# A fused two-block transformer kernel: x is loaded and normalised ahead of the memory, whose transposes move between the first four token groups

## What is computed

```python
# first block (mixer 0), L = 256 tokens, D = 2048
sh1, sc1, g1, sh2, sc2, g2 = split(silu(c) @ w_mod + b_mod, 6)        # w_mod: 2048 x 12288
h = rms_norm(x, norm_g[0]) * (1 + sc1) + sh1
y = real(fftn(h.reshape(L, 8, 256), axes=(0, 2))) @ fnet_w_out        # Fourier mixing
x = x + g1 * rms_norm(y, norm_g[1])
x = x + g2 * rms_norm(sqrelu_mlp(modulate(rms_norm(x, norm_g[2]), sh2, sc2)), norm_g[3])
# second block, the part that needs only the inputs
mn = rms_norm(mem, mem_norm_g)                                        # mem: 256 x 2048
mk, mv = split(mn @ w_mem_kv, 2)                                      # w_mem_kv: 2048 x 1024
```

## Time and profile before

| | |
|---|---|
| three runs, median (lowest to highest) | 2219.46 us (2216.54 to 2219.74) |
| the profiled execution, its own time | 2221.41 us |
| its span in the profile | 2219.7 us |
| TensorE busy | 2156.7 us (97%) |
| VectorE busy | 1324.4 us (60%) |
| ScalarE busy | 972.6 us (44%) |
| mean granted TensorE clock over the span | 0.98 of full |

### The profile page before, as it was taken

How to read it: one execution, slowest core, us unless ns; L and a number is a source line. 1 busy time by engine, 2 the same in 40 slices (tenths; PEclk the granted TensorE clock), 3 DMA queues, 4 the chain that set the end, 5 groups by cost and what they waited for, 6 DMA issues and landing times.

```text
span 2219.7 us, 31332 instructions
## 1 busy us (share of the span) xinstructions
PE 2156.7 (97%) x11753; PEld 1823.6 (82%) x11753; DVE 1324.4 (60%) x1318; ACT 972.6 (44%) x1134; POOL 45.2 (2%) x69
## 2 busy tenths in 40 slices
PE   5999988999999999999999999999999999999999
PEld 3867867888888888888979879888888888888887
DVE  3568976655655565656766547655645554655563
ACT  4244435343434443434534446754534343443342
POOL 0000000000000000001000000000000000000000
PEclk9889989999999999999999989999999999999999
DMA  9899996667667667666655535556656656656654
GB/s 388 287 404 347 390 372 203 210 220 214 209 213 214 211 213 219 207 210 206 209 145 151 145 97 145 198 185 186 192 191 190 187 192 189 188 190 190 188 189 151
DMA packets 219188, 478.98 MB, mean 216 GB/s; under 512 B 14708, under 2 KB 15084, under 8 KB 218336
## 3 DMA queue, kind: packets, MB, share of 16 engines
q1 hardware_dynamic: 211940, 450.98, 63.0%
q0 software_dynamic: 6480, 25.69, 3.7%
q10 hardware_dynamic: 684, 1.14, 0.1%
HBM read 472.50 MB, written 5.24 MB: 215 GB/s over the span
## 4 chain that ended last, share of the span: by engine, by line
PE 90%; DVE 4%; DMA 3%; ACT 2%; issue 1%; SPq 0%; DVEq 0%; ACTq 0%
PE ps L443 21%; PE ps L461 13%; PE ps L463 13%; PE ps L462 13%; PE ps L444 11%; PE ps L447 3%; PE ps L448 3%; PE ps L449 3%; DMA raw<-in_w_mod_dram 1%; DVE acc L1351 1%; PE ps L509 1%; DMA raw<-in_w_in_dram 1%; PE ps L487 1%; DVE wl L1326 1%; PE ps L799 1%
## 5 line engine op out<-in xcount | busy, mean ns | idle before, releaser
L1326 DVE TENSOR_TENSOR wl<-raw,wh 128x1024 fp32r<-128x1024 f32 x688 | 812.2, 1220 | 333.2 <-ACT wh L949 332.1
L949 ACT ACTIVATE wh<-raw 128x1024 fp32r<-128x1024 f32 x688 | 699.8, 1054 | 539.1 <-DMA raw<-in_w_down_dram 161.5
L443 PE MATMUL ps<-xt,wh 128*128 128x512 f32 x2048 | 724.8, 399 | 9.0 <-DVE wl L1326 9.0
L444 PE MATMUL ps<-xt,wl 128*128 128x256 f32 x2048 | 576.2, 281 | 0.0
L443 PEld LDWEIGHTS ps<-xt,wh 128*128 128x128 f32 x2048 | 386.1, 189 | 105.5 <-issue 10.7
L461 PE MATMUL ps<-wh,u 128*128 128x512 f32 x1120 | 436.7, 390 | 0.3 <-DVE wl L1326 0.3
L462 PE MATMUL ps<-wl,u 128*128 128x512 f32 x1120 | 435.8, 389 | 0.0
L463 PE MATMUL ps<-wh,u 128*128 128x512 f32 x1120 | 435.8, 389 | 0.0
L444 PEld LDWEIGHTS ps<-xt,wl 128*128 128x128 f32 x2048 | 388.6, 190 | 0.3
L461 PEld LDWEIGHTS ps<-wh,u 128*128 128x128 f32 x1120 | 210.2, 188 | 44.9 <-issue 0.8
L463 PEld LDWEIGHTS ps<-wh,u 128*128 128x128 f32 x1120 | 210.2, 188 | 43.8
(11 more groups left out here) (287 smaller groups left out, 1579.3 us busy)
## 6 DMA issues: line engine op xcount, KB each, us to landing
raw<-in_w_mod_dram SPq DMA_DIRECT2D x160, 512.0 KB, 8.1
raw<-in_w_mlp_in_dram SPq DMA_DIRECT2D x128, 512.0 KB, 3.8
raw<-in_w_mlp_out_dram SPq DMA_DIRECT2D x128, 512.0 KB, 4.7
raw<-in_w_up_dram SPq DMA_DIRECT2D x128, 512.0 KB, 3.8
raw<-in_w_down_dram SPq DMA_DIRECT2D x128, 512.0 KB, 3.7
raw<-in_w_in_dram SPq DMA_DIRECT2D x96, 512.0 KB, 3.7
raw<-in_fnet_w_out_dram SPq DMA_DIRECT2D x32, 512.0 KB, 5.2
slot<-in_w_mod_dram POOLq DMA_DIRECT2D x32, 512.0 KB, 4.7
```

The costliest lines, as they stand in the source:

```text
L443: mm(o, a, flat(xt[:, kt, :, :]), start=first, stop=end, skip_group_check=True)
L444: last = mm(o[:, 0:S], b, xt[:, kt, 0, :], start=False, stop=end, skip_group_check=True)
L949: A(flat(wh[:, i, :, :]), raw[:, landed[0], :], ACT.Copy).then_inc(sem("w_hi"), 1)
L1326: V.tensor_tensor(flat(wl[:, s, :, :]), raw[:, s, :], flat(wh[:, i, :, :]).bitcast(F32), ALU.subtract).then_inc(sem("w_lo"), 1)
```

## The change

Loads: `x` goes first, and the memory behind eight modulation tiles. ScalarE squares and normalises `x` first, writes `xn` and `dfth`, and only then squares the memory (with a scratch tile of its own, `mjunk`). VectorE makes the low parts of `xn` and `dftl` at once. On TensorE no round of transposes stands ahead of the first token group any more; the four rounds stand behind the token groups 0, 1, 2 and 3. In VectorE's loop the low parts of the rounds 0 and 1 stand ahead of the tiles 12 and 14.

```diff
--- before.py
+++ after.py
@@ -111,6 +111,7 @@
 
         xn = at("xn", [P, 2, HALVES, D], F32R, O_U)
         junk = at("junk", [P, D], F32, O_U)
+        mjunk = at("mjunk", [P, D], F32, O_XT + 16 * KB)
         acc2 = at("acc2", [P, D], F32, O_U + 16 * KB)
         x1t = at("x1t", [P, KT, S], F32, O_U)
         mkt = at("mkt", [P, 4, S], F32, O_Y)
@@ -284,11 +285,12 @@
             def weight(w, i, col):
                 return rows(w)[:, 2 * i:2 * i + 2, col:col + GC]
 
-            sp.dma_start(y[:, :, :], mem[0].rearrange("(a p) d -> p a d", p=P)).then_inc(sem("mem_in"), 16)
+            sp.dma_start(h[:, :, :], x[0].rearrange("(a p) d -> p a d", p=P)).then_inc(sem("x_in"), 16)
             row_loads(sp, 1)
-            sp.dma_start(h[:, :, :], x[0].rearrange("(a p) d -> p a d", p=P)).then_inc(sem("x_in"), 16)
             for n in range(MODN):
                 load(C_SC1 + n, mod_view(1, n))
+                if n == 2 * QUAD - 1:
+                    sp.dma_start(y[:, :, :], mem[0].rearrange("(a p) d -> p a d", p=P)).then_inc(sem("mem_in"), 16)
             for m in range(2 * CH):
                 load(chunk_c(m), weight(w_mem_kv, m % CH, (m // CH) * GC))
                 for j in range(2):
@@ -539,23 +541,24 @@
                                       stop=half == 1 and z == 1, skip_group_check=True)
                 last.then_inc(sem("dft_t"), 1)
 
-            transposes(0, y, [0])
             pe.wait_ge(sem("silu_ready"), 2)
             mod_rows("sc1", C_SC1, 0, 0)
             mod_rows("sc1", C_SC1, 4, 0)
-            transposes(0, y, [1])
-            mod_rows("sc1", C_SC1, 8, 0)
             pe.wait_ge(sem("xn_lo"), 2)
             pe.wait_ge(sem("dft_lo"), 1)
             for g in range(6):
                 dft_tokens(g)
+                if g == 0:
+                    mod_rows("sc1", C_SC1, 8, 0)
+                    transposes(0, y, [0])
                 if g == 1:
+                    transposes(0, y, [1])
+                if g == 2:
                     pe.wait_ge(sem("rows_folded"), 1)
                     mod_rows("sc1", C_SC1, 16, 0)
                     transposes(0, y, [2])
-                if g == 2:
+                if g == 3:
                     mod_rows("sc1", C_SC1, 20, 0)
-                if g == 3:
                     transposes(0, y, [3])
             mod_rows("sc1", C_SC1, 24, 0)
             pe.wait_ge(sem("rows_folded"), 2)
@@ -980,25 +983,24 @@
             act.wait_ge(sem("vt_ready"), 1)
             A(vtmp[:, :], v("c", KT), ACT.Exp, scale=-1.0).then_inc(sem("c_exp"), 1)
 
-            act.wait_ge(sem("mem_in"), 16)
             act.wait_ge(sem("const_set"), 2)
-            for a in range(HALVES):
-                A(junk[:, :], y[:, a, :], ACT.Square, accum_out=ssq[:, a, 0:1]).then_inc(sem("sq"), 1)
-                act.wait_ge(sem("sq"), a + 1)
+
+            def squares(src, scratch, landed, n0):
+
+                act.wait_ge(sem(landed), 16)
+                for a in range(HALVES):
+                    A(scratch[:, :], src[:, a, :], ACT.Square, accum_out=ssq[:, a, 0:1]).then_inc(sem("sq"), 1)
+                    act.wait_ge(sem("sq"), n0 + a + 1)
+
+            squares(h, junk, "x_in", 0)
             root(1)
             act.wait_ge(sem("rs_ready"), 1)
-            act.wait_ge(sem("x_in"), 16)
-            for a in range(HALVES):
-                A(junk[:, :], h[:, a, :], ACT.Square, accum_out=ssq[:, a, 0:1]).then_inc(sem("sq"), 1)
-                act.wait_ge(sem("sq"), 3 + a)
-            root(2)
-            xt_hi(0, v("mem", KT), (0,))
-            act.wait_ge(sem("rs_ready"), 2)
             A(xn[:, 0, 0, :], h[:, 0, :], ACT.Copy, scale=rstd[:, 0:1]).then_inc(sem("xn_hi"), 1)
             act.wait_ge(sem("consts_in"), 16 * N_CONSTS)
             A(dfth[:, :, :], dft_raw[:, :, :], ACT.Copy).then_inc(sem("dft_hi"), 1)
             A(xn[:, 0, 1, :], h[:, 1, :], ACT.Copy, scale=rstd[:, 1:2]).then_inc(sem("xn_hi"), 1)
-            xt_hi(0, v("mem", KT), (1,))
+            squares(y, mjunk, "mem_in", 2)
+            root(2)
 
             def tok_out(g):
                 act.wait_ge(sem("dft_t"), g + 1)
@@ -1012,8 +1014,8 @@
                     hi_static(0)
                     hi_static(1)
                 tok_out(g)
-                if g in (1, 3):
-                    xt_hi(0, v("mem", KT), (2 + g // 2,))
+                if g < 4:
+                    xt_hi(0, v("mem", KT), (g,))
             for m in range(2, CH + 4):
                 hi_static(m)
                 if m == 8:
@@ -1405,9 +1407,6 @@
             dve.wait_ge(sem("silu_ready"), 1)
             V.tensor_copy(silu32[:, :, :], siluc[:, :].rearrange("p (k o) -> p k o", o=1).to_broadcast([P, KT, QP])).then_inc(sem("silu_ready"), 1)
             mean(1, 1, "sq", 2)
-            diagonals()
-            mean(1, 2, "sq", 4)
-            dve.wait_ge(sem("acc0_seeded"), 16)
             def normed_lo(a):
 
                 dve.wait_ge(sem("xn_hi"), a + 1)
@@ -1415,16 +1414,20 @@
                                        in1=xn[:, 0, a, :].bitcast(F32), op0=ALU.mult,
                                        op1=ALU.subtract).then_inc(sem("xn_lo"), 1)
 
+            normed_lo(0)
+            dve.wait_ge(sem("dft_hi"), 1)
+            V.tensor_copy(flat(lmask[:, :, :]), lmask_raw[:, :])
+            V.tensor_tensor(dftl[:, :, :], dft_raw[:, :, :], dfth[:, :, :].bitcast(F32),
+                            ALU.subtract).then_inc(sem("dft_lo"), 1)
+            normed_lo(1)
+            mean(1, 2, "sq", 4)
+            diagonals()
+            dve.wait_ge(sem("acc0_seeded"), 16)
+
             for n in range(MODN):
-                if n == 6:
+                if n == 12:
                     xt_lo_round(0, 0, v("mem", KT))
-                    normed_lo(0)
-                    dve.wait_ge(sem("dft_hi"), 1)
-                    V.tensor_copy(flat(lmask[:, :, :]), lmask_raw[:, :])
-                    V.tensor_tensor(dftl[:, :, :], dft_raw[:, :, :], dfth[:, :, :].bitcast(F32),
-                                    ALU.subtract).then_inc(sem("dft_lo"), 1)
-                    normed_lo(1)
-                if n == 12:
+                if n == 14:
                     xt_lo_round(0, 1, v("mem", KT))
                 if n == 20:
                     xt_lo_round(0, 2, v("mem", KT))
```

## The result

| | before | after |
|---|---|---|
| median of ten runs (lowest to highest) | 2220.24 us (2216.54 to 2221.47) | 2224.55 us (2221.59 to 2225.69) |
| ratio of the times, 95% interval | | 1.0019 (1.0011 to 1.0027) |
| span of the profiled execution | 2219.7 us | 2223.1 us |

The changed kernel is slower by 4.3 us, 0.19%. The forecast was +4.2 us, to 2223.7 us; the 0.8 us that this median lies above it come from the kernel before, whose median was 2219.46 us over three runs and 2220.24 over ten.

What follows compares the result with a forecast made beforehand. TensorE, busy 97% of the span, was taken as the bound, the opening set by the first chunk's start. Order +3.7 and clock +0.5 gave +4.2 us on the 2219.46 us median: 2223.7 us, range 2216 to 2229.

Steps and rivals of the forecast that it cites:

- The loads: Opening loads: tiles 3 and 7 land 5.4 us earlier, memory at 27.4, tile 8 onward as before; slots freed earlier gain nothing.
- x first: Opening: x is normalised first, token group 0 starts at 26.7 us and is hidden by tile 11's landing.
- the sentence on the cover: Token group 0: a later DFT matrix has 0.5 to 3.3 us of cover; beyond that it costs one for one.
- The memory's diagonals: ScalarE's work on the memory, landing at 27.4: diagonals there at about 34.0 us, with nothing waiting for them yet.
- Round 0, tiles 12 to 15, the fold: Deciding steps: round 0 follows tiles 8 to 11, low parts delay the first fold to 50.0, tiles 16 to 19 to 50.2.
- The order's term: Start of the first chunk: tiles 16 to 19 later, less token group 2 already done (2.8 us); net +3.7 us.
- The clock: Around tiles 16 to 19: a longer TensorE wait costs somewhat more at the lower clock; +0.5 us, bounds nothing to 2.8.
- a clock term of 0: Trainium skill's alternative: a restart counts, not the wait's length beyond that, so the sum would be 3.7 us.
- What comes later: Behind the first chunk, from 70 us: TensorE's and the loads' chains both start 3.7 us later.
- The cold start: Tiles 8 to 11 and round 0 run at the lower clock, fold 3 to 3.5 us later; 2227 us, chance 0.13.
- Absorption: A chain between 70 and 341 us not hanging on the first chunk ends last, shift vanishes; 2219.5 us, chance 0.12.
- the early fold: First fold done before tile 19 lands at 43.6 us, group 2 fills TensorE's wait; 2214.8 us, chance 0.11.

Runs made afterwards that it cites:

- e3: Changed kernel with the memory loaded behind four modulation tiles instead of eight; ratio to the kernel before 1.0019.
- e6: Changed kernel with the loads back in the order of the kernel before (memory, x, tiles), engine orders as changed; 2222.14 us, ratio to the kernel before 1.0014.
- e5: Changed kernel with VectorE's low part of round 1 moved behind the first fold, second run of that kernel; 2217.24 us, ratio to the kernel before 0.9991.
- e12: Changed kernel with round 1's low part done once more on VectorE, into unused SBUF, between the products of tiles 13 and 14; ratio to the kernel before 1.0028.
- e9: The changed kernel once more, unaltered, for a second profile and more times; ratio to the kernel before 1.0021.
- e10: The kernel before once more, unaltered, for a second profile; ratio to the kernel before 1.0000.
- e7: Changed kernel with 15 small matmuls on the identity in TensorE's wait ahead of the memory's first chunk; ratio to the kernel before 1.0016.
- e1: Changed kernel with VectorE's low part of round 1 behind the first fold instead of between tiles 13 and 14; ratio to the kernel before 0.9983.
- e2: Changed kernel with 18 small matmuls on the identity in TensorE's wait ahead of tiles 16 to 19; ratio to the kernel before 1.0017.
- e4: Changed kernel with tiles 12 to 15 and the first fold ahead of every low part, rounds 1 to 3 one place later; 2212.77 us, ratio to before 0.9969.
- e11: The order of e4 with 10 small matmuls ahead of tiles 8 to 11 and 4 ahead of the first chunk; 2214.70 us, ratio to the kernel before 0.9973.
- e8: Kernel before with 12 small matmuls in the wait ahead of tiles 16 to 19 and 15 ahead of the first chunk; ratio to the kernel before 0.9984.

## Why the prediction was right, point by point

**The loads.** Right: tile 11 landed at 32.83 (32.8 said), the memory at 27.4, x early enough. Nothing was gained by slots that come free earlier. What was overlooked is the gap from 60 to 62 us: the prediction followed the loads of tiles 26 to 31 and not the one behind them, which takes tile 20's slot. The first chunk did not wait for it.

**x first.** Right: token group 0 started at 26.87 (26.7), ran partly cold to 31.5 and was hidden by the landing of tile 11. In e3 and e6 this cover was gone, and the start of tiles 8 to 11 moved by 1.6 and 3.2 us, as the sentence on the cover says. The memory's diagonals were done at 32.7, not 34.0: from the first square to the reciprocal root it took 4.8 us, not 6.1, since ScalarE's table load of 1.28 us ahead of the first root (16.53) does not come again ahead of the second. Nothing waited for them, as said.

**Round 0, tiles 12 to 15, the fold.** This is the step that decides, and it was right: fold at 48.40 (48.8 said), tiles 16 to 19 at 49.68 (50.2). e5 (low part behind the fold, 2.8 us earlier) and e12 (low part twice, 1.62 us later) show it as the cause. The order's term was a little too large: 49.68 - 43.74 - 2.8 = 3.1 us, not 3.7. I had put a step of 5.5 us for each round, read from round 1 of before, whose transposes took 2.31 us; here they took 2.0, and the steps 5.4 and 5.3. Tiles 14 and 15 took 2.7 us instead of 2.8, and TensorE started 0.04 us behind the fold instead of 0.2.

**The clock.** The direction was right, the size too small: +0.5 us was taken. Tiles 16 to 19 and round 2 took 3.64 + 2.90 = 6.5 us instead of 2.44 + 3.08 = 5.5, so +1.0; the second profiles repeat both (6.5 in e9, 5.5 in e10). The length of the wait alone doesn't set this: behind the same 4.5 us it was 6.2 us in e3, 5.4 in e6 and 5.3 in e7, and behind the 6.05 us of e12 5.8. In e9, e7 and e1 tiles 8 to 11 ran cold as well (3.44, 3.00 and 3.31 us), another 1.1 to 1.5 us, which I had mostly discounted ("they now follow a token group"). It is between group 0 and tile 11 that TensorE waits: 3.0 us in e9, where the group ran at the full clock and ended at 29.6, and 1.5 us in the profile after, where it ran partly cold and tiles 8 to 11 took 1.92. Order and clock together give 3.1 + 1.0 = 4.1 us, against 74.10 - 69.92 = 4.2 measured. The two errors cancel: that 4.2 us was hit so closely is luck, the mechanism is not.

The prediction set the sum with a clock term of 0 beside its own. For the two kernels it is too small, by 1.0 us; e6 and e7, whose restart cost no more than that of before, agree with it. The rule of the Trainium skill ("TensorE: Matmul & The Clock Gate", section "HAM oscillation — how this bites in real kernels") that a wait puts the clock back and the next burst starts cold agrees with 3.64 against 1.92 us (e2).

**What comes later.** "Nothing absorbs it" holds for this pair: 4.2 us at the first chunk, 3.4 in the spans, 4.3 in the medians. As a rule it is not shown: e2 and e7 gained 2.1 to 2.5 us at or behind the first chunk and under 1 us in the time, though their intervals just reach the full gain; e6 lost 2.0 us there and nothing in the time; and e1 and e5 gained more in the time than in front of the first chunk. Part of that is the clock of 66 to 100 us, which the two profiles of before and the two of after have alike at 0.80, and so cancels in their comparison.

**The rivals.** The cold start was half right: tiles 8 to 11 ran cold in some executions, the changed kernel's own e9 among them, and the fold came 1.2 us later there, not 3 to 3.5; round 0 took 2.0 us in every profile of the changed kernel and its variants but e1's and e7's (2.25 and 2.55). Absorption and the early fold did not happen; but the early fold's own rule, that TensorE's wait is filled if the fold comes before 43.6, is what e4 makes true, and it turns the sign.

**What stays open.** What sets the clock behind the first chunk. From the profiles alone (0.80 in all four of the two kernels, 0.85 to 0.95 in the others, e6 with its late first chunk among them) one can't tell order from chance. The timed executions say more: the mean granted clock over the whole span was 0.9812 and 0.9814 in the changed kernel (10 executions each), 0.9808 in e3 and 0.9810 in e12 (11 and 9), but 0.9845 in e6 and 0.9847 and 0.9834 in e1 and e5 (11, 12 and 11), with standard errors of at most 0.0006; the kernel before had 0.9817 to 0.9824. In e6 the profiles put 0.0009 of the 0.0033 above the changed kernel ahead of 66 us (0.95 against 0.92 there) and 0.0023 between 66 and 100. So it goes with the kernel and is not the luck of one profile, although the order of work behind the first chunk is the same in all of these. Through which step an earlier or later opening changes the clock behind it is not shown.

## What to carry to other kernels

Before moving a transfer or a stage ahead to fill a wait, look for the in-order queue that must pass through the moved work: here VectorE's low part of a round, placed between two products, held a fold that TensorE needed, and 1.7 us of work made 2.8 us of a wait of 4.5. Work that nobody needs soon belongs behind the signal that releases the next engine. Moving that one call turned a loss of 0.2% into a gain of 0.17% (e1) or 0.09%, within noise (e5); moving all rounds behind the folds gave 0.3% (e4). Judge a shift at a landmark of the trace first, and only then by the total: the first low part repeats within 0.03 us (before, e4 and e11), 1.1 us (after and e9) and 1.5 us (e1 and e5), while the total also carries what the clock does behind them.

## What was not expected of the hardware

The granted clock behind the first chunk differs between kernels whose order there is the same: 0.80 to 0.95 of full from 66 to 100 us, 13.6 to 3.4 us at 1.2 GHz, worth some 3 us (34.5 against 31.6 us from the first low part to the third fold, after and e6). Part of it follows 32 matmuls of one column each: 6.8 us at the lower clock in both profiles of both kernels, none in e1 and e6. Small matmuls on the identity that cut a wait from 4.50 to 0.49 us (e2) and from 3.08 to 0.67 us (e8) held 2.4 GHz across it: tiles 16 to 19 took 1.92 us behind the fill in e2 and e8, against 3.64 and 2.44 without it.
